# Up projections of two layers: ten of eleven chunks as seven half products

## The reference, cut to what matters

```python
xn = rms_norm_2(h, ffn_norm[layer])            # 512 x 1024
val, gate = jnp.split(xn @ w_up, 2, axis=-1)   # 512 x 2816 each
gp = jnp.pad(gate, ((0, 0), (CONV_W - 1, 0), (0, 0)))
gc = conv_b + conv_w[0] * gp[:, 0:seq]
for j in range(1, CONV_W):
    gc = gc + conv_w[j] * gp[:, j:j + seq]
h = h + (jax.nn.silu(gc) * val) @ w_down
```

## Time and profile before

| what | us |
|---|---|
| median of three runs (2288.4 to 2290.53) | 2288.41 |
| span of the profiled execution, first to last instruction | 2287.9 |
| TensorE busy in it | 2236.4 |
| VectorE busy | 1255.1 |
| ScalarE busy | 990.6 |
| GpSimd busy | 360.9 |
| mean granted TensorE clock, share of full speed | 0.993 |

### The profile page before, as it was taken

How to read it: one execution, slowest core, us unless ns; L and a number is a source line. 1 busy time by engine, 2 the same in 40 slices (tenths; PEclk the granted TensorE clock), 3 DMA queues, 4 the chain that set the end, 5 groups by cost and what they waited for, 6 DMA issues and landing times.

```text
span 2287.9 us, 30159 instructions
## 1 busy us (share of the span) xinstructions
PE 2236.4 (98%) x11479; PEld 1806.6 (79%) x11479; DVE 1255.1 (55%) x2250; ACT 990.6 (43%) x1835; POOL 360.9 (16%) x432
## 2 busy tenths in 40 slices
PE   7899999999999999999989999999999999999999
PEld 6677777788877787878878888888888668888887
DVE  6966565756645454544493555464444565454543
ACT  7445655533554545463432423333344664232322
POOL 7742131126202030300000000000034000000000
PEclk9999999999999999999999999999999999999999
DMA  7354212134232222225462232322222302322232
GB/s 224 118 170 129 74 56 93 43 105 157 101 112 68 87 80 87 86 71 176 164 213 89 78 111 79 106 92 85 100 92 92 130 20 74 111 92 93 93 101 83
DMA packets 184559, 236.70 MB, mean 103 GB/s; under 512 B 29565, under 2 KB 110932, under 8 KB 184418
## 3 DMA queue, kind: packets, MB, share of 16 engines
q1 hardware_dynamic: 160462, 207.73, 28.1%
q10 hardware_dynamic: 23956, 27.04, 3.7%
HBM read 215.84 MB, written 23.10 MB: 104 GB/s over the span
## 4 chain that ended last, share of the span: by engine, by line
PE 88%; DVE 7%; ACT 2%; issue 1%; POOL 1%; DMA 1%; SPq 0%; ACTq 0%; DVEq 0%; POOLq 0%
PE G L2211 25%; PE G L2213 25%; PE G L2212 25%; DVE w_lo L1762 1%; PE X L2220 1%; PE X L2331 1%; PE X L2342 1%; PE X L2319 1%; PE X L2358 1%; PE X L2345 1%; PE G L2365 1%; PE G L2379 1%; PE X L2315 1%; PE X L2230 1%; POOL small L1172 1%
## 5 line engine op out<-in xcount | busy, mean ns | idle before, releaser
L2211 PE MATMUL G<-w_hi,u_hi 128*128 128x512 f32 x1536 | 622.5, 405 | 4.0 <-issue 2.1
L2213 PE MATMUL G<-w_hi,u_lo 128*128 128x512 f32 x1536 | 601.2, 391 | 0.0
L2212 PE MATMUL G<-w_lo,u_hi 128*128 128x512 f32 x1536 | 599.8, 391 | 0.0
L1762 DVE SCALAR_TENSOR_TENSOR w_lo<-raw,par,w_hi 128x512 fp32r<-128x512 f32 x496 | 373.6, 791 | 402.5 <-ACT w_hi L1250 399.6
L1250 ACT ACTIVATE w_hi<-raw,par 128x512 fp32r<-128x512 f32 x496 | 318.2, 714 | 342.3 <-PE G L2213 339.2
L2211 PE MATMUL G<-u_hi,w_hi 128*128 128x512 f32 (+1 forms) x1168 | 458.2, 392 | 0.3 <-DVE w_lo L1762 0.2
L2213 PE MATMUL G<-u_hi,w_lo 128*128 128x512 f32 (+1 forms) x1168 | 446.0, 382 | 0.0
L2212 PE MATMUL G<-u_lo,w_hi 128*128 128x512 f32 (+1 forms) x1168 | 445.8, 382 | 0.0
L2211 PEld LDWEIGHTS G<-w_hi,u_hi 128*128 128x128 f32 x1536 | 289.1, 188 | 70.1 <-issue 8.7
L2213 PEld LDWEIGHTS G<-w_hi,u_lo 128*128 128x128 f32 x1536 | 288.8, 188 | 62.3
L2212 PEld LDWEIGHTS G<-w_lo,u_hi 128*128 128x128 f32 x1536 | 289.5, 188 | 59.2 <-issue 1.9
(11 more groups left out here) (315 smaller groups left out, 2334.4 us busy)
## 6 DMA issues: line engine op xcount, KB each, us to landing
raw<-in_ffn_w_up SPq DMA_DIRECT2D x88, 512.0 KB, 4.7
raw<-in_e_w_in SPq DMA_DIRECT2D x56, 512.0 KB, 4.7
raw<-in_o_w_in SPq DMA_DIRECT2D x56, 512.0 KB, 4.5
raw<-in_ffn_w_down SPq DMA_DIRECT2D x40, 512.0 KB, 4.3
raw<-in_e_w_out SPq DMA_DIRECT2D x16, 512.0 KB, 4.6
raw<-in_o_w_out SPq DMA_DIRECT2D x16, 512.0 KB, 4.2
raw<-in_a_w_glu SPq DMA_DIRECT2D x16, 512.0 KB, 4.9
raw<-in_w_kv SPq DMA_DIRECT2D x16, 512.0 KB, 4.7
```

The source lines that it names most:

```text
L1762: V.scalar_tensor_tensor(w_lo[:, n % HL, k], raw[:, n % RAW, k], gain(name, k0 + k), w_hi[:, n % HL, k].bitcast(F32), ALU.mult, ALU.subtract)\
L2211: pe.matmul(out, lh, rh, start=start, stop=False)
L2212: pe.matmul(out, lh, rl, start=False, stop=False)
L2213: return pe.matmul(out, ll, rh, start=False, stop=stop)
```

## The change

Of the eleven chunks, the first stays as it was and the other ten become one stage, `seven`. With the tokens' two halves (columns) and the input features' two halves as A11, A12, A21, A22, and a chunk's weights as B11 (first features, gate or value half), B12, B21, B22, each half 128 x 4 x 256, a chunk is made by seven products of halves in place of eight, in Winograd's form. Four products need sums of tokens (S1 to S4), four need sums of weights (T1 to T4); the results are joined from seven products.

- Token sums are made once per layer by VectorE during the first chunk, after two joins of high and low parts and four copies by ScalarE; they too are split in high and low.
- Weight sums are made in SBUF by transfers: SyncE loads B11 into a buffer `growing` (two, by parity of the chunk), and GpSimd issues transfers with `accum_op=ALU.add` that add B12 (T1), B22 (T2) and B21 (T4) in place, one after another, each after the low part of the sum before is done. T3 has a buffer of its own (`border_sum`), B12 with B22 added. Three plain halves are loaded into `raw`. A chunk has five loads and four adds of 512 KB, where it had four loads.
- ScalarE makes the high part of each half (128 x 1024 in one instruction), VectorE the low part, into a ring of four halves made of the two weight buffers. ScalarE also takes four products out of PSUM, VectorE joins others onto them, runs the convolution from SBUF, and multiplies.
- The norm's gain moves from the weights to the tokens: `rms_tiles` multiplies a tile by the row factor and by the gain's vector in one instruction; the vector is loaded once per layer.
- The counts of blocks and the choice of weight buffers, which went by the unit's number, now come from lists (`bb`, `wb`).

```diff
+SEVEN = 10
+PRODUCTS = (("A11", "B11"), ("S1", "T1"), ("A12", "B21"), ("S2", "T2"), ("S4", "B22"), ("S3", "T3"), ("A22", "T4"))
...
-                gains.append((f"ffn{layer}", k0))
+                gains.append(None)
...
         def plan_ffn(layer):
-            plan_tile_norm()
-            plan_chunks([("up", "T", dict(dst=2 * c, layer=layer)) for c in range(11)])
-            first_y = ("y", plan[-10].i, 3)
-            plan_down(22).first_y = first_y
+            plan_tile_norm(layer)
+            plan_chunks([("up", "T", dict(dst=0, layer=layer))])
+            s = plan_seven(layer)
+            plan_down(22).first_y = ("s_y", s.i, 0)
+            plan[-1].seven = s
...
+        def half_tile(o):
+            return att[:, o:o + 2, :].rearrange("p a (b n) -> p (a b) n", n=256)
+        def growing(j):
+            return half_tile(2 * (j % 2))
+        border_sum = half_tile(4)
...
+            def half_load(s, j, name, free):
+                if j:
+                    sp.wait_ge(*at_("sw_done", s.i, 7 * (j - 1) + free))
+                else:
+                    n = s.n + RAW_HALF[name][0] - RAW
+                    sp.wait_ge(w_hi_done, hi_before[n + 1])
+                    sp.wait_ge(w_lo_done, lo_before[n + 1])
+                sp.dma_start(weight_half(s, j, name), quarter(s, j, name)).then_inc(half_loaded[name], 16)
+            def growing_load(s, j):
+                if j >= SEVEN:
+                    return
+                if j >= 2:
+                    sp.wait_ge(*at_("sw_done", s.i, 7 * (j - 2) + 6))
+                sp.dma_start(growing(j), quarter(s, j, "B11")).then_inc(growing_loaded[j % 2], 16)
+            def border_load(s, j):
+                if j:
+                    sp.wait_ge(*at_("sw_done", s.i, 7 * (j - 1) + 5))
+                sp.dma_start(border_sum, quarter(s, j, "B12")).then_inc(border_loaded, 16)
+            def seven_loads(s):
+                half_load(s, 0, "B11", 0)
+                sp.wait_ge(*at_("u_ready", s.norm.i, TT - 1, 1))
+                growing_load(s, 0)
+                half_load(s, 0, "B21", 2)
+                half_load(s, 0, "B22", 4)
+                border_load(s, 0)
+                growing_load(s, 1)
+                for j in range(1, SEVEN):
+                    half_load(s, j, "B11", 0)
+                    half_load(s, j, "B21", 2)
+                    half_load(s, j, "B22", 4)
+                    border_load(s, j)
+                    growing_load(s, j + 1)
...
+            def pool_seven(s):
+                def onto_growing(j, name):
+                    if j >= SEVEN:
+                        return
+                    if name == "B12":
+                        pool.wait_ge(*growing_at(s, j))
+                    elif name == "B22":
+                        pool.wait_ge(*at_("sw_done", s.i, 7 * j + 1))
+                    else:
+                        pool.wait_ge(*at_("sw_done", s.i, 7 * j + 3))
+                    pool.dma_start(growing(j), quarter(s, j, name), accum_op=ALU.add).then_inc(growing_summed[j % 2], 16)
+                def onto_border(j):
+                    if j >= SEVEN:
+                        return
+                    pool.wait_ge(*border_at(s, j))
+                    pool.dma_start(border_sum, quarter(s, j, "B22"), accum_op=ALU.add).then_inc(border_summed, 16)
+                onto_growing(0, "B12")
+                onto_border(0)
+                for j in range(SEVEN):
+                    onto_growing(j, "B22")
+                    onto_growing(j + 1, "B12")
+                    onto_growing(j, "B21")
+                    onto_border(j + 1)
...
+            def product_high(s, q):
+                if q >= 7 * SEVEN:
+                    return
+                j, p = divmod(q, 7)
+                name = PRODUCTS[p][1]
+                act.wait_ge(*half_at(s, q))
+                act.wait_ge(blocks, s.base + q - 3 if q >= 4 else bb[s.n - 2] + 4 * (q // 2) + 4)
+                r, c = ring(s, q)
+                nc.scalar.activation(w_hi[:, r, :, c], weight_half(s, j, name), ACT.Copy)\
+                    .then_inc(*by("sw_high", s.i, q))
...
+            def act_seven(s):
+                for q in range(7 * SEVEN):
+                    j, p = divmod(q, 7)
+                    product_high(s, q + 3)
+                    if q == 0:
+                        token_high(s, "S3")
+                    if p == 1:
+                        act.wait_ge(blocks, product_at(s, j, 0))
+                        if j >= 2:
+                            act.wait_ge(*at_("s_conv", s.i, j - 2, 1))
+                        nc.scalar.activation(gate_rows(j)[:, :, 0:256], chain_bank(j), ACT.Copy)\
+                            .then_inc(*by("p1", s.i, j))
+                    if p == 2:
+                        act.wait_ge(blocks, product_at(s, j, 1))
+                        nc.scalar.activation(value_rows_of(j)[:, :, 256:512], two(G[:, 2, :]), ACT.Copy)\
+                            .then_inc(*by("p5", s.i, j))
+                    if p == 4:
+                        act.wait_ge(blocks, product_at(s, j, 3))
+                        nc.scalar.activation(value_rows_of(j)[:, :, 0:256], chain_bank(j), ACT.Copy, scale=-1.0)\
+                            .then_inc(*by("u2", s.i, j))
+                    if p == 6:
+                        act.wait_ge(blocks, product_at(s, j, 5))
+                        nc.scalar.activation(gate_rows(j)[:, :, 256:512], chain_bank(j), ACT.Copy)\
+                            .then_inc(*by("u3", s.i, j))
+                    if p == 4 and j:
+                        seven_silu(s, j - 1)
+                    if j == SEVEN - 1 and p == 4:
+                        act.wait_ge(*at_(*s.ahead.first_y))
+                        y_split(s.ahead, 0)
+                    if j == SEVEN - 1 and p == 5:
+                        w_high(s.n + s.nu)
+                w_high(s.n + s.nu + 1)
...
+                        V.scalar_tensor_tensor(xn_view[:, t, :], h[:, t, :], rstd[:, t:t + 1], row_scale,
+                                               ALU.mult, ALU.mult).then_inc(*by("xn_ready", s.i, t))
+                        continue
...
+            def product_low(s, q):
+                if q >= 7 * SEVEN:
+                    return
+                j, p = divmod(q, 7)
+                r, c = ring(s, q)
+                dve.wait_ge(*at_("sw_high", s.i, q))
+                V.tensor_tensor(w_lo[:, r, :, c], weight_half(s, j, PRODUCTS[p][1]), w_hi[:, r, :, c].bitcast(F32),
+                                ALU.subtract).then_inc(*by("sw_done", s.i, q))
...
+            def token_sums(s, b):
+                if b == 0:
+                    for t in (2, 3):
+                        for half in range(2):
+                            dve.wait_ge(*at_("x_copied", s.norm.i, t, half))
+                    token_made(s, "S1", x_copy("A21"), x_copy("A22"), ALU.subtract)
+                    dve.wait_ge(*at_("u_ready", s.norm.i, 1, 1))
+                    seven_join(s, "A11")
+                    dve.wait_ge(*at_("su_made", s.i, "S1"))
+                    dve.wait_ge(*at_("joined", s.i, "A11"))
+                    token_made(s, "S2", token_sum("S1"), x_copy("A11"), ALU.subtract)
+                if b == 1:
+                    seven_join(s, "A12")
+                    dve.wait_ge(*at_("su_made", s.i, "S2"))
+                    dve.wait_ge(*at_("joined", s.i, "A12"))
+                    token_made(s, "S4", token_sum("S2"), x_copy("A12"), ALU.add)
+                    token_made(s, "S3", x_copy("A11"), x_copy("A21"), ALU.subtract)
...
+            def dve_seven(s):
+                for q in range(7 * SEVEN):
+                    j, p = divmod(q, 7)
+                    product_low(s, q + 2)
+                    if q == 0:
+                        token_low(s, "S3")
+                    if j and p == 0:
+                        seven_c21(s, j - 1)
+                    if j and p in (1, 2):
+                        seven_conv(s, j - 1, p - 1)
+                    if p == 3:
+                        dve.wait_ge(blocks, product_at(s, j, 2))
+                        dve.wait_ge(*at_("p1", s.i, j))
+                        gate = gate_rows(j)[:, :, 0:256]
+                        V.tensor_tensor(gate, two(G[:, 3, :]), gate, ALU.add)\
+                            .then_inc(*by("c11", s.i, j))
+                    if j and p == 4:
+                        seven_y(s, j - 1)
+                    if p == 5:
+                        dve.wait_ge(blocks, product_at(s, j, 4))
+                        dve.wait_ge(*at_("u2", s.i, j))
+                        value = value_rows_of(j)[:, :, 0:256]
+                        V.tensor_tensor(value, two(G[:, 2, :]), value, ALU.add).then_inc(*by("c12", s.i, j))
+                    if p == 6:
+                        seven_c22(s, j)
+                    if j == SEVEN - 1 and p == 5:
+                        y_rest(s.ahead, 0)
+                    if j == SEVEN - 1 and p == 6:
+                        w_low(s.n + s.nu)
```

(69 more changed lines are left out.)

272 lines of the change are left out of this document (219 added, 53 removed).

## The result

| | us |
|---|---|
| before, median of 4 runs in this comparison (2288.4 to 2290.53) | 2288.51 |
| after, median of 4 runs (2359.64 to 2372.76) | 2367.0 |
| ratio, 95% interval | 1.034 [1.032, 1.036] |
| span of the profiled execution after | 2365.5 |

The changed kernel is slower by 78.5 us. The forecast was 2333 us, range 2262 to 2410.

What follows compares the result with a forecast made beforehand. TensorE, never idle in the up projection, was taken to bound the kernel; the loop of adds then gave a 238.9 us stage against 217.6 per layer, plus 2 for the norm: 2287.9 became 2332.5, forecast 2333 us, range 2262 to 2410.

Steps and rivals of the forecast that it cites:

- the loop: From T2 of one chunk to T2 of the next: a chunk can't be shorter than 2L + 10.5, 24.1 us; chance 0.48.
- The first rival: The adds hide in the stage of ten chunks, L at most 4.8: 22 us less, 2266 us; chance 0.30.
- the turning point: The L at which the changed kernel is neither faster nor slower than before: 5.6 us.
- The prize: TensorE in the up projection: 20.16 us a chunk against 21.76, 1.6 less, 32.0 us over 20 chunks.
- The fourth rival: 256-column matmuls run at a weight load's pace, 0.188 us each, 31.6 us a chunk: 2487 us; chance 0.03.
- The loop without its adds: The queued ScalarE and VectorE work in the loop from T2 to the next T2: 10.5 us.
- L: Time from a low part's end until the add has landed: 6.8 us, from a range of 3.6 to 13.8.
- the second rival: DMA engines fill up: 21.3 us of their work a chunk; at 0.8 a chunk takes 26.6, 2387 us; chance 0.13.
- The engines' price: DMA engines' time per transfer in a chunk: a load 1.64 us, an add twice that.
- the sum: Whole kernel: 2287.9 + 2 x (238.9 - 217.6) + 2 = 2332.5 us, for the norm 1 us a layer.
- The start: First chunk's VectorE work ends 5 to 6 us late; T1 at +1, T2 at about +10 instead of +8.6.
- VectorE's fit: VectorE's steady work in the stage: 16.6 of 20.2 us a chunk, which fits with little room.

Runs made afterwards that it cites:

- the fastest version: T2 and T4 summed by GpSimd's own addition, with token sums spread over the first chunk's steps, against the version with GpSimd's two sums: 2269.3 us, ratio 0.992.
- The early y: SiLU and y of the chunk before moved ahead of the wait for T4's sum: 2363.1 us against the changed kernel; 2317.7 with three loads left out too.
- GpSimd's sums: T2 and T4 made by GpSimd's own addition in SBUF in place of two adding transfers, against the changed kernel: 2273.0 us, ratio 0.993.

## Why the prediction was right in the main, point by point

**Direction and mechanism: right.** The forecast was the loop, with ScalarE's high parts of T2 and T4 waiting for adds and TensorE idle behind them; the waits show it, and the run without adds has none. The first rival (adds hide, 2266) fell: the fastest of 60 adds landed after 5.7 us, above the turning point of 5.6.

**The prize: right.** Matmuls of 256 columns start 120 ns apart (1355.00, 1355.12, 1355.24 in the timeline of the stage), with a weight load for each. The fourth rival fell.

**The loop without its adds: nearly right.** 10.5 us forecast, 7.6 + 2.3 = 9.9 in the turn above, 9.6 in the mean of nine.

**L: the size nearly right, its nature wrong.** The prediction took one length, 6.8 us. It is 6.1 for the add of B21 and 9.7 for the add of B22 in the turn shown, 6.7 and 8.1 in the mean. The add of B22 goes out together with the add of B12, behind the border's add at 1443.13, and between two loads of SyncE's at 1445.01 and 1448.47. The step that was off is "I take the median load, the second read and 0.5 us for GpSimd": that is an add by itself (5.7 at best, 6.0 in the median with few loads), and nothing in it stands for what else is under way. In place of it the runs showed that the landing grows with other transfers beside it: a median of 6.0 with three loads gone, 7.4 with all, and 6.9 and 9.1 when the rest of the loop is shortened. That a turn came out at 24.5 us against 24.1 is luck in part: the two adds were 1.3 us too short in sum, the rest 0.9 too long. The forecast (24.1 us a chunk) and the second rival (22.0 us of DMA work, at 0.9 of the engines 24.5) come out alike, and the runs show a part of each: three loads less saved about 2 us a chunk, SiLU and y off the loop saved next to nothing with all loads and 0.6 us with three gone. The 0.9 in the second sum was read from the windows after the result; no run shows it to be a bound.

**The engines' price: the rival was right.** It held an add at twice a load, 3.3 us; 3.46 was measured. The Trainium skill, Collectives: The Full Stack, "The bandwidth ceiling: the fold count and why AG ≠ RS ≠ AR", has the reducing step of a ring at half the rate of the copying one; the adding transfers here agree roughly, with a ratio of 3.46 / 1.58 = 2.2. The Trainium skill, DMA: Bandwidth & Descriptors, "Anatomy of one DMA — SWDGE (gpsimd) path", gives by its fit an estimated 3.2 us for 512 KB; the fastest plain transfer of GpSimd took 3.8 and the median 6.3, so here the measurement decides against it.

**Where 33 us were missing.** The change cost 77.6 us of span, the sum had 44.6. For the first layer, counted from 1320.1 (1537.73 less ten chunks of 21.76), the time to T2 was 17.2 us against 10 and 1 for the norm; nine turns took 220.4 against 216.9; the rest to the down projection 15.3 against 12.0. In the second layer, counted from where its first chunk now begins, they were 17.7, 226.0 (25.1 a turn) and 14.5 us. So of the 33 us the starts have 12.9, the eighteen turns 12.6, the ends 5.8, and 1.7 lie between the stages. (The prediction let a us of L weigh 38 us; its 10 us to the first T2 hold one more L in each layer, so by its own terms it is 40.)
- *The start (13 us in two layers, on a forecast of 11 each) is the term sized worst.* "So it ends 5 to 6 us late, and its low part of T1 comes after the chunk's end" was right in time, but the sum put T1 at +1; it came at +6.6 (1325.48 + 1.21 = 1326.69), since the low parts of the first chunk also waited for the token sums. The add behind it took 6.2 us (T2's high part starts at 1332.92), but T2's low part then stood in VectorE's queue behind the low part of S3, which waited for ScalarE, and ended at 1337.32: 4.4 us instead of 2.4.
- *The clock was left out.* The idle times that the sum allows leave TensorE at the lower level for a while. After the 3.27 us at the start, the starts of eight matmuls of 512 columns, from 1315.92 to 1319.30, stand about 0.42 us apart instead of 0.227 (the 1.2 and the 2.4 GHz level), 1.6 us more; over the stage the granted clock is 0.94. The rows below show the two paces.

```profile
1315.38 0.47 PE L2658 MATMUL G<-u_hi,w_hi 128*128 128x512 f32 x1 [3.27 <-DVE w_lo L2084]
...
1317.59 0.63 PE L2658 MATMUL G<-u_hi,w_hi 128*128 128x512 f32 x1
1318.02 0.63 PE L2659 MATMUL G<-u_lo,w_hi 128*128 128x512 f32 x1
...
1320.24 0.39 PE L2660 MATMUL G<-u_hi,w_lo 128*128 128x512 f32 x1
1320.47 0.39 PE L2658 MATMUL G<-u_hi,w_hi 128*128 128x512 f32 x1
```

**VectorE's fit: right.** 16.6 us a chunk forecast; without adds 160.6 of 205 us are 15.8 per 20.16.

**What stays open.** Whether ten chunks could gain the whole 32 us: the fastest version gains 19, and its start still has 3.3 us of idle time in the first layer's window. The early y together with GpSimd's sums wasn't tried, nor a run that takes only the border's add away from the add of B22. Why the second layer's turns are 0.6 us longer than the first's isn't settled.

## What to carry to other kernels

Where a transfer stands between two engines' steps in a closed loop, write the loop down and price the transfer as its length alone plus what else is under way at that moment; a step saved elsewhere moves the transfer closer to the ones before it, and here what was saved came back as landing time, nearly all of it at a DMA share of 0.90 and most of it at 0.76. List every wait of the loop again after a change: a single buffer put a load back into it. Transfers that add are good for sums that nobody waits for; a sum on the path belongs on an engine, if its operands are in SBUF anyway. And a stage that puts its preparations on a half-idle engine must look at the order there: 7 us of new work ahead of one needed instruction stops TensorE however low the engine's mean is.

## What the runs showed of the hardware that was not expected

- An adding transfer of 128 x 4 rows of 1 KB is cut into 528 packets, a plain one of GpSimd's into 144; its issue holds GpSimd's queue for 1.28 us, against 0.75.
- While GpSimd adds two operands from SBUF (2.4 to 2.6 us for 128x1024), VectorE's operations with two inputs in SBUF took 2.25 instead of 1.22 us and 2.78 instead of 0.75.
- An idle time of 3.27 us costs TensorE more than itself: the matmuls of 512 columns behind it start 0.42 us apart instead of 0.227 from 1315.92 to 1319.30.
